# Attention of branch D in a two-layer hybrid block: heads in pairs, values as weights, probabilities divided ahead of the turn

## What is computed

```
sc   = einsum('bqhd,bkhd->bhqk', qb, k) * scale
mask = key_chunk[None, :] <= qch[:, None]
p    = softmax(where(mask, sc, MASK_VALUE), axis=-1)
o    = einsum('bhqk,bkhd->bqhd', p, v)          # (512, 4 * 64)
return o * silu(gate)
```

## Time and profile before

| | |
|---|---|
| median of three runs | 1495.29 us (1494.77 to 1495.38) |
| the profiled execution: time / span | 1494.77 us / 1493.0 us |
| granted TensorE clock, mean | 0.999 of 2.4 GHz |
| TensorE matmul busy | 1470.7 us, 99% of the span |
| VectorE / ScalarE / GpSimd busy | 952.7 / 448.9 / 97.1 us |
| HBM | 80 GB/s over the span |

### The profile page before, as it was taken

One profiled execution on the slowest core, in us unless ns is written; L12 is line 12 of the kernel. 1 busy time (PEld: TensorE's weight loads), 2 busy tenths in 40 slices (PEclk: granted clock), 3 DMA queues, 4 the chain that ended last, 5 costly groups with the idle time before them and its releaser, 6 DMA issues.

```text
span 1493.0 us, 18777 instructions
## 1 busy us (share of the span) xinstructions
PE 1470.7 (99%) x7236; PEld 1089.3 (73%) x7236; DVE 952.7 (64%) x1658; ACT 448.9 (30%) x931; POOL 97.1 (7%) x70
## 2 busy tenths in 40 slices
PE   9999999999999999999999999999999999999997
PEld 7886777888888888888888844555867745556855
DVE  6849476633787666777634258878743477877833
ACT  4674444430121111111100242233443342144432
POOL 0251000000000000000000042000000150000000
PEclk9999999999999999999999999999999999999999
DMA  5211111142213222222223222112142312111132
GB/s 217 84 43 57 57 57 57 57 161 85 71 66 105 85 85 85 85 85 85 85 85 113 80 92 68 43 57 72 45 140 71 122 49 70 43 58 43 58 127 71
DMA packets 38297, 120.10 MB, mean 80 GB/s; under 512 B 4000, under 2 KB 8352, under 8 KB 37696
## 3 DMA queue, kind: packets, MB, share of 16 engines
q1 hardware_dynamic: 37872, 116.66, 23.3%
q0 software_dynamic: 336, 2.23, 0.4%
HBM read 112.58 MB, written 6.29 MB: 80 GB/s over the span
## 4 chain that ended last, share of the span: by engine, by line
PE 90%; DVE 8%; issue 1%; DVEq 1%; DMA 0%; ACT 0%; SPq 0%; ACTq 0%
PE PS L856 19%; PE PS L953 14%; PE PS L923 9%; PE PS L981 5%; PE PS L676 5%; PE PS L527 5%; PE PS L1231 4%; PE PS L800 4%; PE PS L1374 4%; PE PS L1401 3%; PE PS L516 2%; PE PS L632 2%; DVE SC L2822 1%; PE PS L1030 1%; PE PS L770 1%; PE PS L1002 1%
## 5 line engine op out<-in xcount | busy, mean ns | idle before, releaser
L953 PE MATMUL PS<-HN,ring 128*128 128x512 f32 x576 | 258.0, 595 | 0.0
L953 PEld LDWEIGHTS PS<-HN,ring 128*128 128x128 f32 x576 | 107.0, 190 | 121.1 <-issue 118.8
L856 PE MATMUL PS<-SC 128*128 128x257 f32 x624 | 144.1, 380 | 3.2 <-DVEq L2202 3.1
L1736 ACT ACTIVATE SC<-PS 128x257 f32<-128x257 f32 x60 | 23.1, 385 | 375.2 <-PE PS L856 297.0
L856 PEld LDWEIGHTS PS<-SC 128*128 128x128 f32 x624 | 118.1, 190 | 21.4 <-DVEq L2202 4.4
L2822 DVE SCALAR_TENSOR_TENSOR SC<-SC 128x512 f32<-128x512 f32 x120 | 109.7, 914 | 5.8 <-issue 0.5
L856 PE MATMUL PS<-HN,ring 128*128 128x257 f32 x352 | 79.8, 380 | 0.0
L856 PEld LDWEIGHTS PS<-HN,ring 128*128 128x128 f32 x352 | 66.8, 190 | 9.5
L527 PE MATMUL PS<-HN,ring 128*128 128x257 f32 (+1 forms) x320 | 71.6, 383 | 0.0
L527 PEld LDWEIGHTS PS<-HN,ring 128*128 128x128 f32 x320 | 60.4, 190 | 10.1 <-issue 1.1
L1231 PE MATMUL PS<-HN,ring 128*128 128x256 f32 x256 | 56.4, 380 | 0.0
(11 more groups left out here) (568 smaller groups left out, 2665.1 us busy)
## 6 DMA issues: line engine op xcount, KB each, us to landing
ring<-wst SPq DMA_DIRECT2D x188, 512.0 KB, 3.7
outT<-X SPq DMA_DIRECT2D x18, 256.0 KB, 4.5
X<-xT SPq DMA_DIRECT2D x16, 264.0 KB, 5.6
X<-outT SPq DMA_DIRECT2D x16, 256.0 KB, 4.9
V<-small POOLq DMA_DIRECT2D x2, 1024.0 KB, 6.9
outT<-X SPq DMA_DIRECT2D x4, 384.0 KB, 2.6
V<-s5w SPq DMA_DIRECT2D x1, 1280.0 KB, 10.8
consts<-cst SPq DMA_DIRECT2D x1, 1235.5 KB, 13.3
```

The costliest lines, as they stand in the source:

```text
L856: ins = mm(PS[at % 8 // 2][:, at % 2, 0:257], left[:, b * P:b * P + P], right[:, b, :], start=(b == 0), stop=(b == 3))
L953: ins = mm(bank(b), ring[:, r, i * P:i * P + P], HN[:, i, 0:SEQ], start=(i == 0), stop=(i == KD - 1))
```

## The change

Heads are taken in pairs (0 and 1, 2 and 3), block by block. VectorE divides the exponentials by their row sums in `SD` before the turn (`prob`); TensorE's turn waits for that. In the weighing the values (128 keys x 64 columns) become the weights operand and the turned probabilities stream with 128 columns; the two heads of a pair write partitions 0 to 63 and 64 to 127 of bank 5, which holds the pair's whole output (columns by tokens). So `d_out` and `weighed` go, and ScalarE copies bank 5 to `OD` once a pair (`d_weighed`). All three queues get a new order. Score slots in `SD` and banks 2 and 3 go by head now, not by block.

TensorE, the helpers:

```diff
                         ins.then_inc(SEMS[f"ba{2 + x}"], 1)
                 def d_score(h, t):
-                    b = 2 + t % 2
+                    b = 2 + h % 2
                     take(b)
                     mm(bank(b)[:, 0:t * P + P], QF[0:QKR, h, t * P:t * P + P], KF[0:QKR, h, 0:t * P + P],
                        start=True, stop=True).then_inc(SEMS[f"bd{b}"], 1)
-                def d_turn(t):
-                    pe.wait_ge(*n("d_ex"))
+                def d_turn(h, t):
+                    pe.wait_ge(*n("d_prob"))
                     if turned[0]:
                         pe.wait_ge(SEMS["d_wt"], turned[0])
                     turned[0] += 1
                     for b in range(t + 1):
-                        ins = nc.tensor.transpose(bank(4)[:, b * P:b * P + P], SD[:, t, b * P:b * P + P], c("ident"))
+                        ins = nc.tensor.transpose(bank(4)[:, b * P:b * P + P], SD[:, 2 * (t % 2) + h % 2, b * P:b * P + P], c("ident"))
                     ins.then_inc(SEMS["d_tr"], 1)
-                def d_weigh(h, t):
-                    pe.wait_ge(*n("d_wt"))
-                    take(5)
+                def d_weigh(g, t):
+                    pe.wait_ge(*n("d_wt", 2))
+                    if t == 0:
+                        take(5)
                     for b in range(t + 1):
-                        ins = mm(bank(5)[:, 0:64], WD[:, t % 2, b, :], VD[:, b, h * 64:h * 64 + 64], start=(b == 0), stop=(b == t))
-                    ins.then_inc(SEMS["bd5"], 1)
-                def d_out():
-                    pe.wait_ge(*n("d_mul"))
-                    for cc in range(2):
-                        take(2 + cc)
-                        for t in range(4):
-                            ins = nc.tensor.transpose(bank(2 + cc)[:, t * P:t * P + P], OD[:, t, cc * P:cc * P + P], c("ident"))
-                        ins.then_inc(SEMS[f"bd{2 + cc}"], 1)
+                        for x in range(2):
+                            v0 = (2 * g + x) * 64
+                            ins = mm(bank(5)[64 * x:64 * x + 64, t * P:t * P + P], VD[:, b, v0:v0 + 64], WD[:, x, b, :],
+                                     start=(b == 0), stop=(b == t))
+                    if t == 3:
+                        ins.then_inc(SEMS["ba5"], 1)
                 def b_diag():
                     pe.wait_ge(*n("b_mul"))
```

GpSimd's wait, VectorE's helpers and d_end:

```diff
-                pool.wait_ge(*n("d_misc"))
+                pool.wait_ge(*n("d_misc", 3 if l else 1))
...
-                def scores(t):
-                    w_ = t * P + P
-                    got(2 + t % 2)
-                    released(v.tensor_tensor_reduce(SD[:, t, 0:w_], bank(2 + t % 2)[:, 0:w_], c("mlamask", SEQ - w_, w_), 1.0, 3.0e38,
-                                                    ALU.add, ALU.min, sd[:, t:t + 1]), 2 + t % 2)
+                def scores(h, t):
+                    w_, b, k = t * P + P, 2 + h % 2, 2 * (t % 2) + h % 2
+                    got(b)
+                    released(v.tensor_tensor_reduce(SD[:, k, 0:w_], bank(b)[:, 0:w_], c("mlamask", SEQ - w_, w_), 1.0, 3.0e38,
+                                                    ALU.add, ALU.min, sd[:, k:k + 1]), b)
                     mark("d_sc")
-                def weighed(h, t):
-                    got(5)
-                    link(v.reciprocal(sd[:, 8 + t:9 + t], sd[:, 4 + t:5 + t]))
-                    released(ts(OD[:, t, h * 64:h * 64 + 64], bank(5)[:, 0:64], sd[:, 8 + t:9 + t], None, ALU.mult), 5)
+                def prob(h, t):
+                    k = 2 * (t % 2) + h % 2
+                    dve.wait_ge(*n("d_ex"))
+                    link(v.reciprocal(sd[:, 8 + k:9 + k], sd[:, 4 + k:5 + k]))
+                    x = SD[:, k, 0:t * P + P]
+                    ts(x, x, sd[:, 8 + k:9 + k], None, ALU.mult).then_inc(SEMS["d_prob"], 1)
...
                 def d_end():
-                    for cc in range(2):
-                        got(2 + cc)
-                        z = PJ2[:, 26 + cc, :]
-                        released(stt(z, z, 0.5, bank(2 + cc), ALU.mult, ALU.mult), 2 + cc)
-                    mark("y_done")
+                    dve.wait_ge(*n("d_misc", 2))
+                    z = PJ2[:, 26:28, :]
+                    stt(z, z, 0.5, OD[:, :, :], ALU.mult, ALU.mult).then_inc(SEMS["y_done"], 1)
```

More of the change, by code:

```diff
@@ L168, in build @@
             sem(f"bf{b}")
-            if b not in (0, 1, 4):
+            if b not in (0, 1, 4, 5):
                 sem(f"bd{b}")
@@ L1281, in _ @@
                 pe.wait_ge(*n("d_tok"))
-                pe.wait_ge(*n("d_q"))
                 s, uses = n.now("bf4")
                 pe.wait_ge(s, uses)
[L1285 to L1292, removed]
-                        b_level(2)
[L1294 to L1301, removed]
-                        a_mean()
-                    half(6 * h + 2)
-                    if h == 1:
+                for x in range(2):
+                    pe.wait_ge(*n("d_q"))
+                    d_score(x, 0)
@@ new lines, in _ @@
+                for g in range(2):
+                    h0, h1, i0 = 2 * g, 2 * g + 1, 12 * g
+                    half(i0)
+                    if g == 1:
+                        b_level(2)
+                    d_score(h0, 1)
+                    half(i0 + 1)
+                    d_turn(h0, 0)
+                    d_score(h1, 1)
+                    if g == 1:
+                        a_mean()
+                    half(i0 + 2)
+                    if g == 1:
+                        b_level(3)
+                    d_turn(h1, 0)
+                    half(i0 + 3)
+                    if g == 1:
+                        a_var()
+                    d_weigh(g, 0)
+                    d_score(h0, 2)
+                    d_turn(h0, 1)
+                    half(i0 + 4)
+                    if g == 1:
+                        b_level(4)
+                    d_score(h1, 2)
+                    d_turn(h1, 1)
+                    half(i0 + 5)
+                    d_weigh(g, 1)
+                    d_score(h0, 3)
+                    half(i0 + 6)
+                    b_level((0, 5)[g])
+                    d_turn(h0, 2)
+                    d_score(h1, 3)
+                    half(i0 + 7)
+                    d_turn(h1, 2)
+                    half(i0 + 8)
+                    if g == 0:
@@ L1305, in _ @@
                         b_diag()
-                    if h == 2:
-                        b_level(3)
-                    if h == 3:
+                    else:
                         b_level(6)
[L1310 to L1313, removed]
+                    d_weigh(g, 2)
+                    d_turn(h0, 3)
+                    half(i0 + 9)
+                    if g == 0:
                         b_level(1)
-                    if h == 2:
-                        a_var()
@@ L1317, in _ @@
[L1317 to L1325, removed]
-                        a_mix()
[L1327 to L1330, removed]
@@ L1331, in _ @@
-                    if h == 1:
+                        for x in (2, 3):
+                            pe.wait_ge(*n("d_q"))
+                            d_score(x, 0)
+                    d_turn(h1, 3)
+                    half(i0 + 10)
+                    if g == 1:
+                        a_mix()
+                    d_weigh(g, 3)
+                    half(i0 + 11)
+                    if g == 0:
                         b_values()
-                    if h == 3:
+                    else:
@@ L1941, in _ @@
                 mark("b_act")
[L1943 to L1954, removed]
+                for g in range(2):
+                    h0, h1, i0 = 2 * g, 2 * g + 1, 10 + 6 * g
+                    if g == 0:
+                        d_exps(0, 0)
+                        d_exps(1, 0)
+                    d_exps(h0, 1)
+                    evac(i0, (2, 12)[g])
+                    if g == 1:
                         mark("c_in")
-                    d_turned(1)
-                    if h == 2:
+                    d_turned(h0, 0)
+                    d_exps(h1, 1)
+                    d_turned(h1, 0)
+                    if g == 1:
                         act.wait_ge(*n("a_dve"))
-                        af(SQA[:, :, :], CA[:, :, :], ACT.Square).then_inc(SEMS["a_sq"], 1)
+                        af(SQA[:, :, :], CA[:, :, :], ACT.Square).then_inc(SEMS["a_act"], 1)
                         c_tanh(0)
[L1961 to L1971, removed]
+                    evac(i0 + 1, (3, 13)[g])
+                    if g == 1:
                         mark("c_in")
-                    if h == 2:
+                    d_exps(h0, 2)
+                    d_turned(h0, 1)
+                    if g == 1:
                         log_exp()
@@ L1999, in _ @@
                         mark("b_tok")
[L2000 to L2003, removed]
+                    else:
+                        evac_gate(21, 21, 1)
+                        mark("gate_th")
                 for x in range(2):
@@ L2921, in a_squares @@
                 def a_squares():
-                    dve.wait_ge(*n("a_sq"))
```

(12 more changed lines are left out.)

134 lines of the change are left out of this document (77 added, 57 removed).

## The result

The changed kernel takes 1501.7 us (median of 5 runs, 1500.75 to 1503.94) against 1495.38 before: 1.0043 times as long, 95% interval 1.0032 to 1.0055. It was forecast at 1501.5 us. The total is right; the terms behind it are only partly so, and that the two lie 0.2 us apart is luck.

The account below looks back on a forecast made before the run. TensorE, busy 1470.7 of 1493.0 us, was taken as the bound. Work -3.0, old waits -2.2, new waits +8.3 gave +3.1 us a layer, +6.2 in two: 1501.5 us, own range 1498.5 to 1505, over all cases 1489 to 1507.

Parts of the forecast that it names:

- work: TensorE per layer: cheaper weighing passes, 9.2 to 7.1 us, and 0.87 us of d_out turns gone; 3.0 us less.
- old waits: TensorE's waits in the old order of the attention loop, mostly heads 0 and 1, would go: 2.2 us a layer.
- new waits: Six TensorE waits in the second pair, from the fixed queue order of VectorE and ScalarE: 8.3 us a layer.
- No wait in the first pair: Heads 0 and 1: two or more halves stand between each score and its turn, so TensorE would never wait.
- b_level(3): Second pair: TensorE waits for bank 6, freed by VectorE's centring (a_center), 2.3 us a layer.
- a_var: Second pair: TensorE waits for VectorE's squares, which follow pick and next, 0.5 us a layer.
- b_level(4): Second pair: TensorE waits for bank 7, freed by ScalarE's logarithm, 1.0 us a layer.
- b_level(6): Second pair: TensorE waits for VectorE's b_next(5), the end of the longest chain, 2.9 us a layer.
- the walk: Step-by-step timing of three engines' queues in the second pair; under 5 us of waits there would show it wrong.
- The clock: Granted clock taken as 1.00 in the attention loop, no cost; a lower one would show the forecast's queue timing wrong.
- that the waits are small: Rival, second pair: waits stay at the old 2.2 us a layer, saved work counts whole, 1489.3 us; chance 0.20.
- Halves that take turns: Rival, weighing: the array's column halves do not run side by side, 4.2 us more passes a layer, 1507.5 us; chance 0.04.

Follow-up runs that it names:

- The kernel with six moves: Changed kernel with three steps of VectorE's queue reordered, plus VectorE's squares of branch A and two ScalarE steps taken earlier: 1483.68 us, ratio 0.9922.
- work in the waits: Changed kernel plus 8 and 11 useless TensorE multiplications a layer in its two long waits, ahead of b_level(3) and b_level(6): 1498.26 us, ratio 1.0021.
- three moves: Changed kernel, VectorE taking the centring, scores(3, 3), and scores(3, 2) with prob(2, 2) earlier in its queue: 1489.22 us, ratio 0.9958.
- the two with one move: Changed kernel with one VectorE step earlier: centring ahead of conv(0) and prob(3, 1), 1498.28 us; or scores(3, 3) ahead of a_act and side_sum(1), 1493.04 us.
- the first experiment: Changed kernel with VectorE centring branch A ahead of conv(0) and prob(3, 1) instead of behind them: 1498.28 us, ratio 1.0022.

## Why the prediction was right, and where its terms were not

The forecast was +3.1 us a layer as -3.0 work, -2.2 old waits, +8.3 new waits. The kernel with six moves gives the loop without waits: 120.18 us in layer 1 less its 0.41 of waiting, 119.8 (layer 2, with no wait left: 119.82). Against that, in us a layer:

| term | forecast | layer 1 | layer 2 |
|---|---|---|---|
| work and old waits, `d_out` with them | -5.2 | -6.0 (119.8 - 124.94 - 0.86) | -6.0 (119.8 - 124.92 - 0.84) |
| new waits | +8.3 | +6.2 | +5.8 |
| rest: lower clock, and some 0.5 around the waits (129.47 and 127.44, less 119.8, less waits) | 0 | +3.5 | +1.9 |
| together | +3.1 | +3.7 | +1.7 |

With the later start of 0.95 that is 6.3 us, beside 6.2 forecast. The misses cancel: too little work saved and too many new waits were forecast, no lower clock, no later start. That the kernel gets slower through new waits was foreseen; that the figure fits so well is luck.

- **Work**: mis-sized by 0.8. The passes cost what was taken, 0.054 for 0.055, and going in 0.16 for 0.15; but coming out costs 0.10 where 0.19 was taken from a late product, 0.7 us over 8 visits. The rule of the Trainium skill ("TensorE: Matmul & The Clock Gate", Part 3: Packing small matmuls), that a weight load overlaps running multiplications only when the row group differs, does not hold for this form: both heads use all rows, and a pass takes 0.054 us, half of the 0.105 of the old weighing.
- **No wait in the first pair**: right (55.90 of 55.90 us busy).
- **The places of the waits**: right for five of six, with the releasers that were named. Their sizes, forecast and measured in layer 1: `b_level(3)` 2.3 and 2.16, `a_var` 0.5 and none, `b_level(4)` 1.0 and 0.37, weighing of t = 1 0.9 and 0.48, `turn(3, 2)` 0.7 and 0.23, `b_level(6)` 2.9 and 2.97. The two long ones stand. At full clock, with work in the waits, `a_var` has 0.37 and `b_level(4)` 0.94: the walk was right there for a clock of 1.00, and the slow half covered them.
- **The clock**: the step that failed. The prediction took TensorE's durations at 1.00 throughout and named a lower clock in the loop as what would show the walk wrong. It was there, and it cost 2.5 us in the loops of the profiled execution (3.4 between the medians), which the work in the waits gave back. The 5.4 in the table is more for two reasons. The kernel with work in the waits, at a clock of 1.00, has such a rest too, some 0.5 us a layer (127.44 less 119.8 less waits of 7.16 in layer 1, the filled ones counted at their old length), so that part is not the clock; and the later waits that the slow halves covered, 0.37 + 0.57 a layer, took back 1.9.
- **VectorE's divisions**: `prob` was put at 0.5 us a block; by starts it takes 0.47 for 256 columns. Making it short gave some 1.3 us in all, with single runs that overlap.
- **Rivals**: that the waits are small did not come by itself; moving steps made it so. Its forecast, 1489.3 us with waits left at some 2.2 us a layer, is what three moves gave: 1489.2 with 2.75 and 2.4 us, where a larger saving of work stands against the longer waits and the later start. Halves that take turns were put at 4.2 us of passes a layer; at 0.054 us a pass they do not, and taking the heads one behind the other costs 1.5.

## What to carry to other kernels

When a bottleneck engine loses work, look at which fixed queues now decide when it may go on, and walk them step by step: the saving here (6 us a layer, the old waits included) was there all along, and moving six steps in two other queues that have idle time turned 0.4% slower into 0.8% faster. Price a new wait as long as the ones here (1.8 us and more) by the clock that may follow it as well, not by its own length alone. A move pays only when it stands ahead of the last thing the waiting engine needs; the next wait is often one step behind it, so moves are tried together.

## What the runs showed of the hardware

- The granted clock fell to the lower level behind some waits and not behind others of the same length. In the six kernels without work in the waits and with a long wait left (the changed one, the two with one move, the one with three, the two with the weighing or the division altered), 18 waits of 1.8 us or more stand in the profiled loops; behind 12 of them instructions run at the lower clock, behind 6 they do not. 1.81 us ahead of `a_var` had it in the first experiment and not in the third, 2.97 us ahead of `b_level(6)` had it in the changed kernel and not with the heads one behind the other, both in layer 1. Behind waits under 1 us it never came, nor behind the two of 1.46 and 1.47 us. What decides between them stays open. The five times of the changed kernel spread over 3.2 us, the slowest at a mean clock of 0.992 and the fastest at 0.996; those of the kernel with six moves, at 0.998 and 0.999, spread over 0.9.
- Multiplications by the identity in a wait kept the clock at 1.00 and paid: 38 more of them, 2.5 us less in the two loops and 3.4 between the medians.
- Column halves of the array run side by side though the turns stand two multiplications apart: 0.66 us for t = 1 in either order. Three and four multiplications of a head in a row cost more, 1.15 for 0.88 us and 1.58 for 1.09.
